# Paired partial-array matmuls in linear attention and key sums, with two heads gated inside the last unit

## What is computed

```python
# gated linear attention, 4 heads, key width 128, value width 256, chunks of 64 tokens
log_a = log_sigmoid(g_low @ w_gate + b_gate) / 16      # g_low has 16 columns
cum = cumsum(log_a within the chunk); tot = cum[last]
s = where(mask, (q*exp(cum)) @ (k*exp(-cum)).T, 0)
o = s @ v + (q*exp(cum)) @ state
state = exp(tot) * state + (k*exp(tot-cum)).T @ v
y = (rms_norm(o per head) * norm_g * silu(r)) @ w_out
# forgetting attention, 8 heads of width 64
c = cumsum(log_sigmoid(fg + b_forget), over tokens)
p = softmax(q @ k.T / 8 + c[query] - c[key], causal); out = p @ v
```

## Time and profile before

| what | value |
|---|---|
| runs | 1558.78 us median of 3 (1558.70 to 1558.85) |
| profiled execution | 1558.36 us |
| its span | 1556.5 us |
| TensorE busy | 1541.0 us, 99% of the span |
| TensorE weight loads | 1322.8 us, 85%, beside the matmuls |
| VectorE busy | 951.8 us, 61% |
| ScalarE busy | 745.8 us, 48% |
| GpSimd busy | 133.0 us, 9% |
| DMA engines | 182 GB/s on average |
| granted TensorE clock | 0.999 of full |

### The profile page before, as it was taken

How to read it: one execution, slowest core, us unless ns; L and a number is a source line. 1 busy time by engine, 2 the same in 40 slices (tenths; PEclk the granted TensorE clock), 3 DMA queues, 4 the chain that set the end, 5 groups by cost and what they waited for, 6 DMA issues and landing times.

```text
span 1556.5 us, 21118 instructions
## 1 busy us (share of the span) xinstructions
PE 1541.0 (99%) x8516; PEld 1322.8 (85%) x8516; DVE 951.8 (61%) x952; ACT 745.8 (48%) x700; POOL 133.0 (9%) x141
## 2 busy tenths in 40 slices
PE   8999999999999999999999999999999999999998
PEld 7888888788888888889878888898999788888886
DVE  5655565575556655565457665557686456775555
ACT  5454455445444445453334445445536556454442
POOL 1000020120001100023121200002003200020000
PEclk9999999999999999999999999999999999999999
DMA  7554564254554654455444464556444335455552
GB/s 304 189 189 183 193 216 162 109 200 178 205 195 146 223 208 186 188 204 220 172 169 157 152 233 188 186 194 236 145 163 163 110 134 189 149 203 191 191 190 76
DMA packets 41720, 283.70 MB, mean 182 GB/s; under 512 B 5040, under 2 KB 5232, under 8 KB 8752
## 3 DMA queue, kind: packets, MB, share of 16 engines
q1 hardware_dynamic: 37728, 270.55, 47.1%
q0 software_dynamic: 2368, 8.59, 1.6%
q10 hardware_dynamic: 1552, 3.51, 0.7%
HBM read 281.52 MB, written 1.05 MB: 182 GB/s over the span
## 4 chain that ended last, share of the span: by engine, by line
PE 96%; DVE 1%; ACT 1%; POOL 1%; issue 0%; DMA 0%; DVEq 0%; POOLq 0%; ACTq 0%
PE psum L1535 20%; PE psum L1430 18%; PE psum L1433 17%; PE psum L1434 17%; PE psum L1539 11%; PE psum L1475 2%; PE psum L1462 2%; PE psum L1468 2%; PE psum L1442 1%; PE psum L1772 1%; POOL att_p L376 1%; PE psum L1861 0%; PE psum L1915 0%; PE psum L1883 0%; PE psum L1694 0%
## 5 line engine op out<-in xcount | busy, mean ns | idle before, releaser
L825 DVE TENSOR_TENSOR weights_lo<-weights_raw,weights_hi 128x2048 fp32r<-128x2048 f32 x249 | 574.2, 2319 | 362.5 <-ACT weights_hi L403 360.9
L403 ACT ACTIVATE weights_hi<-weights_raw 128x2048 fp32r<-128x2048 f32 (+1 forms) x256 | 483.3, 1890 | 329.8 <-PE psum L1434 190.7
L1535 PE MATMUL psum<-operand,weights_hi 128*128 128x512 f32 x1376 | 327.6, 390 | 0.0
L1535 PEld LDWEIGHTS psum<-operand,weights_hi 128*128 128x128 f32 x1376 | 255.3, 188 | 51.1
L1430 PE MATMUL psum<-weights_hi,hidden_hi 128*128 128x512 f32 x480 | 188.1, 392 | 0.2
L1433 PE MATMUL psum<-weights_lo,hidden_hi 128*128 128x512 f32 x480 | 187.6, 391 | 0.0
L1434 PE MATMUL psum<-weights_hi,hidden_lo 128*128 128x512 f32 x480 | 186.8, 389 | 0.0
L1539 PEld LDWEIGHTS psum<-operand,weights_lo 128*128 128x128 f32 x1376 | 176.4, 191 | 6.7
L1539 PE MATMUL psum<-operand,weights_lo 128*128 128x256 f32 x1376 | 178.5, 283 | 0.0
L1430 PE MATMUL psum<-operand,weights_hi 128*128 128x256 f32 x576 | 164.2, 285 | 0.0
L1433 PE MATMUL psum<-operand,weights_hi 128*128 128x256 f32 x576 | 163.0, 283 | 0.0
(11 more groups left out here) (266 smaller groups left out, 1567.8 us busy)
## 6 DMA issues: line engine op xcount, KB each, us to landing
weights_raw<-in_weights SPq DMA_DIRECT2D x256, 1024.0 KB, 4.8
ln_rows<-in_ln_rows POOLq DMA_DIRECT2D x16, 512.0 KB, 6.7
normalised<-in_x SPq DMA_DIRECT2D x2, 512.0 KB, 6.4
ret_constants<-in_ret_constants ACTq DMA_DIRECT2D x1, 1024.0 KB, 4.8
out<-normalised SPq DMA_DIRECT2D x4, 256.0 KB, 2.0
att_constants<-in_att_constants ACTq DMA_DIRECT2D x1, 576.0 KB, 4.9
gla_w_low<-in_gla_w_low ACTq DMA_DIRECT2D x1, 512.0 KB, 3.5
att_w_small<-in_att_w_small ACTq DMA_DIRECT2D x1, 512.0 KB, 4.0
```

The source lines that it names most:

```text
L403: nc.scalar.activation(w_hi[:, s, whole], raw[:, s, whole], ACT.Copy).then_inc(hi_split, 1)
L825: nc.vector.tensor_tensor(w_lo[:, s, :], raw[:, s, :], w_hi[:, s, :].bitcast(F32), ALU.subtract).then_inc(lo_split, 1)
L1535: mm(banks[b // 2][:, b % 2, :], w_hi[:, slot, cols], x_both[:, c, :, :].rearrange("p a t -> p (a t)"), start=c == 0, stop=False, skip_gro ...
```

## The change

On TensorE, matmuls that use part of the array are ordered in turns between parts. `gate_logits` has head h on rows 32h to 32h+15 (the low-rank input and the gate weights are laid out so, and each head has a bank of its own). `update(0)` and `update(1)` become one loop that alternates chunk 0 (rows 0 to 63) and chunk 1 (rows 64 to 127), with outputs in separate pairs of banks. `from_state(1)` and `from_state(2)` alternate partitions 64 to 127 and 0 to 63. `update(2)` and `from_state(3)` stay single.

The order of the linear attention changes. The paired update stands before the last unit, alone. The hook before its fifth chunk does both `within_chunks`, the paired `from_state` and `update(2)`; a new hook before its seventh does `from_state(3)` and the transposes of heads 0 and 1 of block 0. VectorE gates heads 0 and 1 as soon as the root is there and only the first gate unit is through silu; heads 2 and 3 are multiplied by the root then and by the gate later (`gated_rest`). The transposes and the two `gained` helpers go by halves of the heads within each block, and three of the four transposed pieces are hooks in the first half of the output product. ScalarE's and VectorE's lists follow this order; the split of tile n+12 moves behind states 1 and 2 and that of n+14 behind the first transposed pieces.

For the key sums, the sums by head are made on partitions 0 to 71 (heads repeated eight times and once more), so that rows 0 to 7 and 64 to 71 both hold them; they are split into a high fp32r part (ScalarE) and a low one (VectorE), the identity is copied to fp32r (`a_pick`), and each head's key sum becomes two fp32r matmuls of 8 rows, alternating between rows 0 to 7 and 64 to 71.

Of helpers that are rewritten as a whole only the new lines stand here; the old ones are in the functions printed above.

```diff
-            g_low = sb("gla_low", [GLA_RANK, TOK], F32, ph)
-            g_wg = sb("gla_w_gate", [GLA_RANK, GLA_HEADS * GLA_DK], F32, ph)
+            g_low = sb("gla_low", [P, TOK], F32, ph)
+            g_wg = sb("gla_w_gate", [P, GLA_DK], F32, ph)
...
-            a_lf = sb("att_log_f", [P, 3, TB, HEADS], F32, ph)
-            a_cT = sb("att_minus_cT", [HEADS, TOK], F32, ph)
+            a_lf = sb("att_log_f", [P, 2, TB, HEADS], F32, ph)
+            a_lfs = sb("att_log_f_repeated", [P, TB, HEAD_DIM + HEADS], F32, ph)
+            a_cT = sb("att_minus_cT", [HEAD_DIM + HEADS, 2, TOK], F32R, ph)
+            a_pick = sb("att_pick", [P, P], F32R, ph)
...
-            nc.scalar.activation(g_low[:, :], acc[0:GLA_RANK, 0, 0:TOK], ACT.Copy).then_inc(low_copied, 1)
+            nc.scalar.activation(g_low[:, :], acc[:, 0, 0:TOK], ACT.Copy).then_inc(low_copied, 1)
...
+            def gained_hi(tb, b):
+
+                act.wait_ge(turned, turns["gla"] + 2 * b + tb + 1)
+                for half in range(2):
+                    last = nc.scalar.activation(x_hi[:, 4 * b + half:4 * b + 4:2, tb * P:(tb + 1) * P],
+                                                pairs[b][:, tb, :].rearrange("p (c t) -> p c t", c=4)[:, half::2, :],
+                                                ACT.Copy, scale=g_gain[:, half:half + 1])
+                last.then_inc(turned_hi, 1)
...
             square_sums(0)
+            square_sums(1)
+            gained_hi(0, 0)
             act.wait_ge(weights_used, n + 12)
             nc.scalar.activation(g_r[:, :, 512:1024], pairs[1], ACT.Silu).then_inc(pair_free[1], 1)
             gate_copied(5)
+            gained_hi(1, 0)
             split_hi(n + 14)
-            gained_hi(0, pairs[1])
-            square_sums(1)
-            gained_hi(1, pairs[0])
+            for tb in range(TB):
+                gained_hi(tb, 1)
...
-                nc.scalar.activation(a_cT[:, :], acc[0:HEADS, 0, 0:TOK], ACT.Copy, scale=-1.0).then_inc(cT_copied, 1)
+                nc.scalar.activation(a_cT[:, 0, :], acc[0:HEAD_DIM + HEADS, 0, 0:TOK], ACT.Copy, scale=-1.0).then_inc(cT_copied, 1)
...
+            nc.scalar.activation(a_pick[:, :], ident, ACT.Copy).then_inc(pick_copied, 1)
...
-                last = nc.vector.tensor_scalar(g_z[:, h, :], acc[:, 1 + h // 2, (h % 2) * TOK:(h % 2 + 1) * TOK],
-                                               g_bg[:, h:h + 1], None, ALU.add)
+                last = nc.vector.tensor_scalar(g_z[:, h, :], acc[:, h, 0:TOK], g_bg[:, h:h + 1], None, ALU.add)
...
-                src = (block_acc(1) if c == 0 else pairs[0]).rearrange("p a (b v) -> p (a b) v", b=2)
+                src = (block_acc(1), block_acc(0), pairs[0])[c].rearrange("p a (b v) -> p (a b) v", b=2)
...
+                head = lambda h: (slice(h * GLA_DV, (h + 1) * GLA_DV), acc[:, 2 * tb + h // 2, (h % 2) * GLA_DV:(h % 2 + 1) * GLA_DV],
+                                  rstd[:, 4 * tb + h:4 * tb + h + 1])
+                for h in range(2, 4):
+                    cols, src, root = head(h)
+                    last = nc.vector.tensor_scalar(g_v[:, tb, cols], src, root, None, ALU.mult)
+                mark(last)
+                dve.wait_ge(unit_copied, 1)
+                for h in range(2):
+                    cols, src, root = head(h)
+                    last = nc.vector.scalar_tensor_tensor(out=g_v[:, tb, cols], in0=src, scalar=root, in1=g_r[:, tb, cols],
+                                                          op0=ALU.mult, op1=ALU.mult)
+                last.then_inc(mixed, 1)
+
+            def gated_rest():
+
+                dve.wait_ge(dve_step, step[0])
                 dve.wait_ge(unit_copied, 2)
+                for tb in range(TB):
+                    cols = slice(2 * GLA_DV, 4 * GLA_DV)
+                    nc.vector.tensor_tensor(g_v[:, tb, cols], g_v[:, tb, cols], g_r[:, tb, cols], ALU.mult).then_inc(mixed, 1)
+
+            def gained_lo(tb, b):
+
+                dve.wait_ge(turned_hi, turns["gla"] + 2 * b + tb + 1)
+                for half in range(2):
+                    part = lambda t: t[:, 4 * b + half:4 * b + 4:2, tb * P:(tb + 1) * P]
                     last = nc.vector.scalar_tensor_tensor(
+                        out=part(x_lo), in0=pairs[b][:, tb, :].rearrange("p (c t) -> p c t", c=4)[:, half::2, :],
+                        scalar=g_gain[:, half:half + 1], in1=part(x_hi).bitcast(F32), op0=ALU.mult, op1=ALU.subtract)
+                last.then_inc(operand_ready, 1)
...
-            split_lo(n + 12)
...
             state(0)
+            state(1)
+            split_lo(n + 12)
             split_lo(n + 13)
-            state(1)
+            state(2)
             gated_output(0)
-            state(2)
-            gained_lo(0, pairs[1])
+            gained_lo(0, 0)
+            gated_output(1)
+            gated_rest()
+            gained_lo(1, 0)
             split_lo(n + 14)
-            gated_output(1)
-            gained_lo(1, pairs[0])
+            for tb in range(TB):
+                gained_lo(tb, 1)
...
-            nc.vector.scalar_tensor_tensor(out=a_lf[:, 2], in0=a_lf[:, 0], scalar=0.0, in1=a_lf[:, 1],
-                                           op0=ALU.min, op1=ALU.subtract).then_inc(lf_ready, 1)
+            repeated = lambda t: t.rearrange("p (r h) -> p r h", r=1).to_broadcast([P, HEAD_DIM // HEADS + 1, HEADS])
+            for tb in range(TB):
+                last = nc.vector.scalar_tensor_tensor(
+                    out=a_lfs[:, tb, :].rearrange("p (r h) -> p r h", h=HEADS), in0=repeated(a_lf[:, 0, tb, :]),
+                    scalar=0.0, in1=repeated(a_lf[:, 1, tb, :]), op0=ALU.min, op1=ALU.subtract)
+            last.then_inc(lf_ready, 1)
...
+            dve.wait_ge(cT_copied, 1)
+            nc.vector.scalar_tensor_tensor(out=a_cT[:, 1, :], in0=acc[0:HEAD_DIM + HEADS, 0, 0:TOK], scalar=-1.0,
+                                           in1=a_cT[:, 0, :].bitcast(F32), op0=ALU.mult, op1=ALU.subtract).then_inc(cT_split, 1)
...
+                            if (tb, s, k, half) in hooks:
+                                hooks[tb, s, k, half]()
...
-                    last = mm(acc[:, 1 + h // 2, (h % 2) * TOK:(h % 2 + 1) * TOK], g_wg[:, h * GLA_DK:(h + 1) * GLA_DK],
-                              g_low[:, :], start=(h % 2 == 0), stop=True, skip_group_check=True)
+                    rows = slice(32 * h, 32 * h + GLA_RANK)
+                    last = mm(acc[:, h, 0:TOK], g_wg[rows, :], g_low[rows, :], start=True, stop=True, skip_group_check=True)
...
+            def update(*chunks):
+
                 for h in range(GLA_HEADS):
+                    for c, out in chunks:
+                        rows, tb = slice((c % 2) * CHUNK, (c % 2 + 1) * CHUNK), c // 2
+                        last = mm(out[:, h // 2, (h % 2) * GLA_DV:(h % 2 + 1) * GLA_DV],
+                                  g_kend[rows, tb, h * GLA_DK:(h + 1) * GLA_DK], g_v[rows, tb, h * GLA_DV:(h + 1) * GLA_DV],
+                                  start=(h % 2 == 0), stop=True, skip_group_check=True)
+                        if h == GLA_HEADS - 1:
+                            last.then_inc(upd_ready, 1)
...
+            def from_state(*chunks):
+
                 for h in range(GLA_HEADS):
+                    for c in chunks:
+                        rows, tb = slice((c % 2) * CHUNK, (c % 2 + 1) * CHUNK), c // 2
+                        last = mm(gla_out(tb, h)[rows], g_qT[:, h, c * CHUNK:(c + 1) * CHUNK], g_state[:, c - 1, h, :],
+                                  start=False, stop=True, skip_group_check=True)
+                        if c % 2 and h % 2:
+                            last.then_inc(gla_o, 1)
+
+            def first_three_chunks():
+                pe.wait_ge(state_ready, 2)
+                for tb in range(TB):
+                    within_chunks(tb)
+                from_state(1, 2)
                 pe.wait_ge(pair_free[0], 3)
+                update((2, pairs[0]))
+
+            def turn_gated(tb, half):
+                pe.wait_ge(mixed, 2 * half + tb + 1)
+                for j in range(4):
+                    c = 4 * half + j
+                    ins = nc.tensor.transpose(pairs[half][:, tb, j * P:(j + 1) * P], g_v[:, tb, c * P:(c + 1) * P], ident)
+                ins.then_inc(turned, 1)
+
+            def last_chunk():
+                pe.wait_ge(state_ready, 3)
+                from_state(3)
+                turn_gated(0, 0)
+
+            def turn_second_half():
+                pe.wait_ge(pair_free[1], 3)
+                for tb in range(TB):
+                    turn_gated(tb, 1)
...
-            update(0, block_acc(1))
-            within_chunks(0)
+            update((0, block_acc(1)), (1, block_acc(0)))
             pe.wait_ge(pair_free[1], 2)
-            tokens_unit(n + 10, pairs[1], between={4: second_chunk})
-            pe.wait_ge(state_ready, 2)
-            update(2, pairs[0])
-            from_state(2)
-            for turn_bank in turn_rows("gla", g_v, 0, pairs[1], mixed, lambda b: 1):
```

(57 more changed lines are left out.)

42 lines of the change are left out of this document (6 added, 36 removed).

## The result

| | before | after |
|---|---|---|
| median of the runs compared | 1559.58 us (6 runs, 1558.70 to 1561.08) | 1548.57 us (6 runs, 1547.95 to 1549.47) |
| ratio, 95% interval | | 0.9926 (0.9916 to 0.9936) |
| profiled execution | 1558.36 us | 1548.65 us |
| its span | 1556.5 us | 1546.8 us |
| TensorE busy | 1541.0 us | 1532.2 us |

The change is faster, by 9.7 us between the two profiles and by 11.0 us between the medians. The forecast was 9.14 us.

A forecast was written before the change was run, and what follows sets the result against it. TensorE's own instruction stream, busy 1541.0 of 1556.5 us, was taken as the bound. Savings of 0.86, 1.72, 1.60, 1.32 and 3.64 summed to 9.14, giving 1549.64 us from the median 1558.78; 8-in-10 range 1548.2 to 1552.0.

The forecast's parts named there:

- gate logits: Linear attention: four calls on four row groups drop from 1.92 to 1.06 us, saving 0.86; bounds nothing and 1.44.
- updates: Linear attention: state updates of chunks 0 and 1, alternating row halves, drop from 3.84 to 2.12 us, saving 1.72.
- reads: Linear attention: state reads for chunks 1 and 2, alternating column halves, take 2.14 us together, saving 1.60.
- waits: Linear attention: the 1.06 us wait for `gla_v` and 0.26 before block 1's first product both go, saving 1.32.
- key sums: Second block: paired fp32r records of 0.068 us cut 5.82 to 2.18 us, saving 3.64; without pairing 1.98.
- Transitions: Tiling-mode borders around hooks: nothing added, because hook pieces showed no extra like the 0.43 us matmul after the gate logits.
- the covers: Reordered linear attention: other engines' work finishes before TensorE asks, with spares of 0.6 to 2.2 us, so reordering costs nothing.
- the bound I chose: Key sums: lower bound of 0.068 us per paired 256-column fp32r record, from paired 128-column attention logits; upper bound 0.12.
- more overlap than half, and borders count: Linear attention: three fewer borders save 0.60 us, four groups at once 0.58 more; 1548.5 us, chance 0.18.
- The slower rival: All paired blocks: each row or column group change drains 0.20 us and nothing overlaps; 1567.9 us, chance 0.03.
- a new wait: Linear attention: TensorE waits at third state, gated block or product's start, about 2 us more; 1551.6 us, chance 0.14.

The follow-up runs named there:

- the sums part alone: Kernel before with only the second block's part of the change (repeated log-forgets, split sums, fp32r key sums in turns): 1554.9 to 1556.3 us, ratio 0.9972.
- the run with late gating: Changed kernel with block 0's last gating step and its transposes moved back behind the last linear-attention unit: 1555.75 us, ratio 0.9972.

## Where the prediction was wrong

The step that failed is the one from the sum to a time. The forecast takes "the median of the runs, 1558.78" as the price of the kernel before, and the sum has no term for the granted clock. The runs show that this median of three lay wholly in the lower of two groups of runs. Three of the six runs in the result, and 27 of the 50 later ones, are 2.0 to 2.4 us longer, and the one profile of that group has the clock at its lower level for 3.4 us right behind the last key sums, at 1.55 us. The change took this second group away: none of its six runs has it, and the kernel with the sums part alone has none in eight. So the measured gain is 11.0 us between the medians, and the ratio, 0.9926, is 11.5 us on 1558.78, where the forecast had 9.14. Against the lower group alone (1558.5) it is 9.9. I had read the first profile for waits and blocks; with three runs and that profile nothing pointed at a second group, and what the old key sums do to the clock was a term at nothing.

The mechanisms of the sum were right (calls on different parts of the array overlap, the waits go), and most of its terms were too small. By its steps:

| step | predicted, us | measured, us |
|---|---|---|
| gate logits | 0.86 | 1.92 - 0.64 = 1.28 |
| updates | 1.72 | 3.84 - 1.93 = 1.91 |
| reads | 1.60 | 3.74 - 1.88 = 1.86 |
| waits | 1.32 | 1.32 - 0.08 = 1.24 |
| key sums | 3.64 | 5.82 - 2.36 = 3.46 |
| together | 9.14 | 9.75 |

That 9.75 is near the 9.7 between the profiles is in part chance. The table leaves out what borders saved (0.41 in the linear attention, see below) and that the profiled run of the change was 0.38 us late at the gate logits (216.30 against 215.92), mostly by a longer start of the program.

**Gate logits** were the step mis-sized most. I took the middle "because each call's two records share a group and must follow each other, as in the logits". That is the price of two groups, 1.06, as the run with two groups shows; four groups overlap further, to 0.64, although each call's two records still share a group. The Trainium skill's figure of 3.07 for four row tiles ("TensorE: Matmul & The Clock Gate", Part 3) would have given 0.63, and the trace agrees with it: 1.92/0.64 = 3.0.

**Updates and reads.** I scaled the price of a block of eight records, 0.133 a record, to sixteen. That price holds a fixed part for the border ahead of the block, which I so counted twice. Sixteen records in turns cost 1.93 and 1.88, the price of one block of eight on one part: a full halving.

**Transitions** I put at nothing, since rows 4 "follow with no such extra". That reading was wrong. Sixteen records within chunks in one block behind full matmuls take 3.45, 0.216 a record; eight by themselves would be 1.73, and the 1.92 and 1.87 in rows 4 hold 0.19 and 0.14 more each. An estimate from these rows, 0.2 for a border and 0.216 for each record that must follow another, gives 1.93 for sixteen records in turns, 1.06 for eight on two groups and 0.63 on four, against 1.93, 1.06 and 0.64. So the borders inside the hook do agree with the drain that I cited there, against what I wrote of them. In the linear attention the layer got 6.70 us shorter and its four lines of the table hold 6.29; the other 0.41 is the products within chunks (3.84 - 3.45 = 0.39) and other borders, less two new ones of 0.20 behind the updates.

**Waits.** All the covers held. Where I had the third state 1.1 us early it was 1.3 early (VectorE done at 275.84, TensorE asking at 277.11), gated block 0 was 1.6 early against 1.2, gated block 1 1.6 against 0.8, since POOL's first instruction took 0.20 and not the 1.20 it had beside a weight split. The tightest was the one I had as the tightest, the first operand of the output product: VectorE was done at 282.01, 0.3 ahead of its matmul at 282.32, where I had 0.6. That matmul takes 0.31 for 0.23; the profile lists no wait there, and what the 0.08 is stays open. The two waits of 0.3 and 1.1 us stayed, as said.

**Key sums.** 256 columns of fp32r took 0.083 a record and not the 0.068 of the bound I chose; the 128-column ones 0.065.

**The rivals.** The first, "more overlap than half, and borders count", was the nearest. Four groups gave 0.42 more than my term where it had 0.58, and fewer borders gave part of its 0.60, as the 6.70 us show. The slower rival had a price on changes of row group; sixteen records in turns, which change group with every call, cost no more than eight on one, so it was wrong outright. Of the ways it could have gone wrong, a new wait is priced by the run with late gating: 4.0 us of wait cost 5.6 in the profile and 7.2 by the medians.

## What to carry to other kernels

Small matmuls that use part of TensorE's rows or columns cost a full matmul each when they stand alone and half or a third when neighbours use other parts; in every such pair here the outputs were in other banks or partitions. Put the neighbours within about four records of each other, and use four row groups where 32 rows are enough. When a block's price is scaled to a longer one, take the border ahead of it out first (here about 0.2 us). Ask also of each wait or few-row stretch on TensorE what the granted clock does behind it: 4.0 us of wait cost 5.6 in the profile. Before a forecast is made from three runs, look whether the kernel's times fall in two groups.

## What the runs showed of the hardware that I had not expected

- Overlap without turns: 4 + 4 fp32r records of different row groups, one block behind the other, took 0.67 us, as in turns; 8 + 8 took 1.54 against 1.04 in turns and 1.93 on one group. For full precision (256 columns) 8 + 8 took 2.90 against 1.93 in turns and 3.84 for twice the single block.
- Eight records of 16 rows and 256 columns: 1.92, 1.06 and 0.64 us on one, two and four row groups.
- A block at which TensorE changes between all rows and columns, part of the rows and part of the columns costs 0.14 to 0.20 us more at its start, also where no 0.43 stands in the chain: products within chunks took 1.92 for eight records behind an update and 3.45 for sixteen behind full matmuls.
- The granted clock fell behind a block of sixteen full-precision records on eight rows in some executions and not in others of the same kernel, at a cost of 1.55 us in the profile that has it; with fp32r or with turns no run showed it.
- With 4.0 us of waiting in two pieces, 0.67 us of transposes between them, the clock was at its lower level from 286.8 to 290.3, and seven matmuls took 3.23 us in place of 1.61.
